# High products first where a stage starts beside the split of its activations

## The reference

```python
def first_block(x, ...):
    for l in range(DEPTH):                                  # DEPTH = 2
        n = rmsnorm(h, attn_norm[l])
        proj = n @ w_in[l]                                  # u, v_sgu, q, k, v_att
        y_sgu = sgu_mixer(gelu(u), gelu(v_sgu), ...)
        y_att = diff_attention(q, k, v_att, ...)
        h = h + concatenate([y_sgu, y_att]) @ w_out[l]
        h = h + conv_ffn(rmsnorm(h, ffn_norm[l]), w_up[l], conv_w[l], conv_b[l], w_down[l])
    return rmsnorm(h, final_norm)

def second_block(x, c, ...):
    h = modulate(rms_norm(x, pre_norm_mix), sh1, sc1)
    y = hybrid_mixer(h, w_in, ..., w_out)                   # concatenate([rnn, att]) @ w_out
    x = x + (1.0 + g1) * rms_norm(y, post_norm_mix)
    h = modulate(rms_norm(x, pre_norm_mlp), sh2, sc2)
    y = square(relu(h @ w_ff1)) @ w_ff2
    return x + (1.0 + g2) * rms_norm(y, post_norm_mlp)
```

## Time and profile before

| what | value |
|---|---|
| median of 3 runs | 1791.74 us |
| lowest and highest | 1791.13, 1794.27 us |
| the profiled execution's own time | 1788.96 us |
| its span, first to last instruction | 1787.2 us |
| TensorE busy | 1754.7 us, 98% of the span |
| weight loads (beside the matmuls) | 1432.7 us, 80% |
| VectorE, ScalarE, GpSimd busy | 63%, 44%, 58% |
| granted TensorE clock | 0.999 |

### The profile page before, as it was taken

The page is one execution under the profiler, slowest core; times in us unless marked ns, Lnnn a source line. Parts: engine busy times, 40 slices in busy tenths (PEclk is TensorE's granted clock), DMA queues, the critical chain, the costliest instruction groups (busy, mean ns, idle before and its releaser), DMA issues. The chain is left out here.

```text
span 1787.2 us, 26072 instructions
## 1 busy us (share of the span) xinstructions
PE 1754.7 (98%) x8977; PEld 1432.7 (80%) x8977; DVE 1123.3 (63%) x1827; ACT 779.9 (44%) x1271; POOL 1033.4 (58%) x1264
## 2 busy tenths in 40 slices
PE   8999999999999999999999999999999999999998
PEld 6876888888888887788888888877666788998886
DVE  4787666666656337766666665654586566666665
ACT  5445443333334335453333333456576654333332
POOL 6584555565465558265455564447411568888885
PEclk9999999999999999999999999999999999999999
DMA  7221223443423221133343332412301112233221
GB/s 256 95 104 51 98 88 132 153 162 109 152 94 118 95 98 57 48 107 118 141 164 137 131 119 94 142 50 96 117 1 49 48 53 90 99 115 116 97 95 47
DMA packets 103206, 184.70 MB, mean 103 GB/s; under 512 B 7322, under 2 KB 67404, under 8 KB 101068
## 3 DMA queue, kind: packets, MB, share of 16 engines
q1 hardware_dynamic: 102940, 183.44, 29.2%
q10 hardware_dynamic: 176, 0.07, 0.0%
HBM read 180.35 MB, written 2.10 MB: 102 GB/s over the span
## 5 line engine op out<-in xcount | busy, mean ns | idle before, releaser
L1003 POOL TENSOR_TENSOR w_lo<-raw,w_hi 128x256 fp32r<-128x256 f32 (+1 forms) x1124 | 908.1, 844 | 729.5 <-ACT w_hi L1087 723.3
L2513 PE MATMUL ps<-n_hi,w_hi 128*128 128x512 f32 (+1 forms) x1320 | 504.6, 382 | 2.0 <-issue 1.6
L2515 PE MATMUL ps<-n_hi,w_lo 128*128 128x512 f32 (+1 forms) x1320 | 499.0, 378 | 0.0
L2514 PE MATMUL ps<-n_lo,w_hi 128*128 128x512 f32 (+1 forms) x1320 | 498.7, 378 | 0.0
L1087 ACT ACTIVATE w_hi<-raw 128x1024 fp32r<-128x1024 f32 (+2 forms) x331 | 307.8, 938 | 356.0 <-PE ps L2515 237.9
L2513 PEld LDWEIGHTS ps<-n_hi,w_hi 128*128 128x128 f32 x1320 | 247.7, 188 | 51.1 <-issue 5.9
L2515 PEld LDWEIGHTS ps<-n_hi,w_lo 128*128 128x128 f32 x1320 | 247.6, 188 | 47.3
L2514 PEld LDWEIGHTS ps<-n_lo,w_hi 128*128 128x128 f32 x1320 | 247.9, 188 | 44.9 <-issue 0.2
L2050 DVE TENSOR_TENSOR ps<-ps,sq 128x512 f32<-128x512 f32 x88 | 61.3, 699 | 178.2 <-PE ps L2515 175.8
L2513 PE MATMUL ps<-x_hi,w_hi 128*128 128x512 f32 x416 | 166.9, 401 | 0.1
L2514 PE MATMUL ps<-x_lo,w_hi 128*128 128x512 f32 x416 | 162.2, 390 | 0.0
(11 more groups left out here) (362 smaller groups left out, 2662.7 us busy)
## 6 DMA issues: line engine op xcount, KB each, us to landing
raw<-in_w_up SPq DMA_DIRECT2D x44, 1024.0 KB, 7.0
raw<-in_w_ff SPq DMA_DIRECT2D x32, 1024.0 KB, 6.6
raw<-in_w_in SPq DMA_DIRECT2D x26, 1024.0 KB, 6.1
zb<-in_ada_w SPq DMA_DIRECT2D x16, 1536.0 KB, 8.5
raw<-in_w_down SPq DMA_DIRECT2D x44, 512.0 KB, 4.0
raw<-in_w_out SPq DMA_DIRECT2D x12, 1024.0 KB, 5.9
raw<-in_w_in SPq DMA_DIRECT2D x4, 512.0 KB, 8.3
za<-in_x SPq DMA_DIRECT2D x4, 512.0 KB, 6.2
```

The lines of the kernel that those rows point to most:

```text
L1003: last = pool.tensor_tensor(part[0], part[1], part[2], ALU.subtract)
L2513: pe.matmul(out, l_hi, r_hi, start=start, stop=False)
L2514: pe.matmul(out, l_hi, r_lo, start=False, stop=False)
L2515: return pe.matmul(out, l_lo, r_hi, start=False, stop=stop)
```

## The change

In the seven starts, a step that was "wait for the low half, then three matmuls for each open output" becomes "wait for the high half; for each open output the two matmuls with the high half; wait for the low half; for each open output the one matmul with the low half". The products and their number are the same, their order within a step is not. In `up` the new helper `pair` does this for two outputs, in `out2` the loop is written out, and the four banks of the first step are waited for together.

```diff
@@ features, for k in range(DT)
-                        pe.wait_ge(lo_ready, split + k + 1)
+                        c = slice(k * P, (k + 1) * P)
+                        pe.wait_ge(hi_ready, split + k + 1)
+                        for t in range(2):
+                            wh, wl = parts[t]
+                            pe.matmul(outs[t][:, :], wh[:, c], n_hi[:, k, :], start=k == 0, stop=False)
+                            pe.matmul(outs[t][:, :], wl[:, c], n_hi[:, k, :], start=False, stop=False)
+                        pe.wait_ge(lo_ready, split + k + 1)
                         for t in range(2):
-                            wh, wl = parts[t]
-                            last = product(outs[t][:, :], ...)
+                            last = pe.matmul(outs[t][:, :], parts[t][0][:, c], n_lo[:, k, :], start=False, stop=k == DT - 1)
                             if k == DT - 1:
                                 last.then_inc(quarter_done, 1)
@@ outa, for k in range(HT)
-                    pe.wait_ge(lo_ready, SPL["sub", l] + k + 1)
+                    pe.wait_ge(hi_ready, SPL["sub", l] + k + 1)
                     for m in range(4):
                         wh, wl = parts[m // 2]
                         c = k * 256 + m % 2 * P
-                        last = product(outs[m][:, :], ...)
+                        pe.matmul(outs[m][:, :], wh[:, c:c + P], n_hi[:, HT + k, :], start=k == 0, stop=False)
+                        pe.matmul(outs[m][:, :], wl[:, c:c + P], n_hi[:, HT + k, :], start=False, stop=False)
+                    pe.wait_ge(lo_ready, SPL["sub", l] + k + 1)
+                    for m in range(4):
+                        c = k * 256 + m % 2 * P
+                        last = pe.matmul(outs[m][:, :], parts[m // 2][0][:, c:c + P], n_lo[:, HT + k, :], start=False,
+                                         stop=k == HT - 1)
                         if k == HT - 1:
                             last.then_inc(quarter_done if m % 2 else full[BK["outa", l, m][0]], 1)
@@ up
+                    def pair(k, hi_made, lo_made):
+                        c = slice(k * P, (k + 1) * P)
+                        wh, wl = [[w_[:, (g + t) % 4, c] for t in range(2)] for w_ in (w_hi, w_lo)]
+                        pe.wait_ge(*hi_made)
+                        for t in range(2):
+                            pe.matmul(ps[t][:, :], wh[t], n_hi[:, k, :], start=k == 0, stop=False)
+                            pe.matmul(ps[t][:, :], wl[t], n_hi[:, k, :], start=False, stop=False)
+                        pe.wait_ge(*lo_made)
+                        for t in range(2):
+                            last = pe.matmul(ps[t][:, :], wh[t], n_lo[:, k, :], start=False, stop=k == DT - 1)
+                            if k == DT - 1:
+                                last.then_inc(quarter_done, 1)
...
-                            pe.wait_ge(lo_ready, split + k + 1)
-                            one(0, k)
-                            one(1, k)
+                            pair(k, (hi_ready, split + k + 1), (lo_ready, split + k + 1))
...
-                            pe.wait_ge(rawlo_ready, RAW[raw] + k + 1)
-                            one(0, k)
-                            one(1, k)
+                            pair(k, (rawhi_ready, RAW[raw] + k + 1), (rawlo_ready, RAW[raw] + k + 1))
@@ out2, for k in range(HT)
+                wh, wl = quarter(STR["out2",].g0 + k // 2)
+                outs = [bank(("out2", 0, t)) if k == 0 else ps[BK["out2", 0, t][0]] for t in range(NT)]
+                c = slice(k % 2 * S, k % 2 * S + S)
+                pe.wait_ge(hi_ready, SPL["att",] + k + 1)
+                for t in range(NT):
+                    pe.matmul(outs[t][:, :], n_hi[:, k, t * P:(t + 1) * P], wh[:, c], start=k == 0, stop=False)
+                    pe.matmul(outs[t][:, :], n_hi[:, k, t * P:(t + 1) * P], wl[:, c], start=False, stop=False)
                 pe.wait_ge(lo_ready, SPL["att",] + k + 1)
                 for t in range(NT):
-                    row_products("out2", ("out2", 0, t), 0, t, k, 1)
+                    last = pe.matmul(outs[t][:, :], n_lo[:, k, t * P:(t + 1) * P], wh[:, c], start=False, stop=k == HT - 1)
...
```

More of the change, by code:

```diff
@@ L2575, in features @@
                     for k in range(DT):
+                        c = slice(k * P, (k + 1) * P)
[4 more added lines that the diff above has]
+                            pe.matmul(outs[t][:, :], wl[:, c], n_hi[:, k, :], start=False, stop=False)
                         pe.wait_ge(lo_ready, split + k + 1)
                         for t in range(2):
-                            wh, wl = parts[t]
-                            last = product(outs[t][:, :], wh[:, k * P:(k + 1) * P], wl[:, k * P:(k + 1) * P],
-                                           n_hi[:, k, :], n_lo[:, k, :], k == 0, k == DT - 1)
+                            last = pe.matmul(outs[t][:, :], parts[t][0][:, c], n_lo[:, k, :], start=False, stop=k == DT - 1)
                             if k == DT - 1:
@@ L2814, in _ @@
                         c = k * 256 + m % 2 * P
-                        last = product(outs[m][:, :], wh[:, c:c + P], wl[:, c:c + P], n_hi[:, HT + k, :],
-                                       n_lo[:, HT + k, :], k == 0, k == HT - 1)
+                        pe.matmul(outs[m][:, :], wh[:, c:c + P], n_hi[:, HT + k, :], start=k == 0, stop=False)
[5 more added lines that the diff above has]
+                                         stop=k == HT - 1)
                         if k == HT - 1:
@@ L3145, in _ @@
             for k in range(HT):
+                wh, wl = quarter(STR["out2",].g0 + k // 2)
[5 more added lines that the diff above has]
+                    pe.matmul(outs[t][:, :], n_hi[:, k, t * P:(t + 1) * P], wl[:, c], start=False, stop=False)
                 pe.wait_ge(lo_ready, SPL["att",] + k + 1)
                 for t in range(NT):
-                    row_products("out2", ("out2", 0, t), 0, t, k, 1)
+                    last = pe.matmul(outs[t][:, :], n_lo[:, k, t * P:(t + 1) * P], wh[:, c], start=False, stop=k == HT - 1)
+                    if k == HT - 1:
+                        if t == NT - 1:
+                            last.then_inc(quarter_done, 2)
+                        else:
+                            last.then_inc(full[BK["out2", 0, t][0]], 1)
                 for f in ((0, 1), (2,), (3, 4), (5, 6))[k]:
```

## The result

| | kernel before | changed kernel |
|---|---|---|
| median, 22 runs each | 1791.07 us | 1793.89 us |
| lowest and highest | 1787.93, 1794.27 | 1791.41, 1798.60 |
| ratio of the medians, 95% interval | | 1.0017 (1.0011 to 1.0023) |
| profiled execution: span | 1787.2 us | 1794.7 us |
| profiled execution: granted TensorE clock | 0.999 | 0.997 |

The change costs 2.8 us, 0.17%; the forecast was 2.6 us, 0.14%, and 1794.3 us (on a median of three runs, which here, over 22, is 0.7 lower). But the two profiled executions lie 7.5 us apart, far more than the medians. So a part of what their traces show is not the change, and most of the experiments are about that part.

A forecast was written before the change was run, and what follows sets the result against it. TensorE, busy 98% of the span, was taken as the bound. Terms -0.51 - 0.27 + 2.72 + 0.65 = +2.59 us gave 1794.3 us on the median, 0.14% slower; range 1790.9 to 1796.4.

The forecast's parts named there:

- out-projection: `outa`, both layers: last step's first tile ends 1.36 us later, passing through a tight chain to `up`; +2.72 us.
- out2: Last step's first tile ends later; row gains shift and the last meets VectorE's second row update; +0.65 us (0 to 0.98).
- x_rnn: Start of `x_rnn`: first product no longer waits for the low half; gain 0.27 us.
- ff1: Start of ff1: first product no longer waits for the low half n_lo; gain 0.51 us.
- up: Start of `up`, both layers: released by GpSimd's w_lo, not the low halves, so gain nothing.
- waits in mid-step: The added wait in the middle of every changed step, already met, keeps the product pace; priced at nothing.
- stall of tile 4: Out-projection: tile 4 waits for tile 0's bank, 0.3 to 0.45 us, lying under the 1.36 us shift.
- the lock: At out2: VectorE and GpSimd lock each other out for a whole instruction; 0.9 us instead of 0.65.
- gains only: Rival: ScalarE or GpSimd catch up with the 1.36 us, leaving -0.78, 1791.0 us; chance 0.15.
- broken stream: Rival: mid-step waits make TensorE restart, 0.09 us in each of 44 steps, 4.0 us on top, 1798.3 us; chance 0.07.
- nothing that matters: Rival: low half almost never late and the tiles' shift absorbed, row updates included; 1791.7 us, chance 0.10.

The follow-up runs named there:

- e6: Kernel before plus a VectorE wait in the seven-products loop and repeated small matmuls before ff1, with the change in `outa` alone; 1791.86 us, ratio 1.0000.
- e7: Kernel before plus a VectorE wait in the seven-products loop and repeated small matmuls before ff1, with the change in out2 alone; 1790.29 us, ratio 0.9990.
- e11: Changed kernel with last steps of outa and out2 tile by tile, plus VectorE's loop wait, without repeated matmuls; 1788.54 us, 0.9977 of kernel before.
- e12: Changed kernel with last steps of outa and out2 tile by tile, VectorE's loop wait and repeated matmuls; 1787.32 us, 0.9964 of kernel before.
- e8: Same kernel as e12, run in an earlier group on the same chip; 1788.30 us, 0.9980 of kernel before.
- e3: Changed kernel plus a wait: VectorE's seventh-quarter low half follows GpSimd's sixth-quarter pieces in the seven-products loop; 1792.61 us, 0.9997 of kernel before.
- e2: Kernel before plus a wait: VectorE's seventh-quarter low half follows GpSimd's sixth-quarter pieces in the seven-products loop; 1789.64 us, ratio 0.9985.
- e1: Kernel before, unchanged, run again; 1792.73 us, ratio 0.9999.
- e9: Same kernel as e2, run again in another group; 1788.86 us, 0.9977 of kernel before.

## Why the prediction was right

The kernel got slower by the amount forecast, and the largest term, the out-projection, came link by link as forecast. The out2 term came near by luck: its amount fits, its collision was another one. Trace sizes come from the shifts of TensorE's starts.

| term | predicted | in the traces | from |
|---|---|---|---|
| out-projection, two layers | +2.72 | +2.61 | 1.32 and 1.29; e6 +3.04 by medians |
| out2 | +0.65 (0 to 0.98) | +0.82 | 2.82 less 2.00 in the table of shifts; e7 +0.84 |
| x_rnn | -0.27 | -0.25 | changed kernel, e11, and -0.27 in e12 |
| ff1 | -0.51 | -0.64 | e11 and e12 |
| up | 0 | 0 | |
| waits in mid-step | 0 | 0 | the pace kept within the changed stages; e8, e12 |
| sum | +2.59 | +2.54 (without falls of the clock) | medians +2.82, and +2.97 (2.3 to 3.6) without the stops |

*Out-projection:* every link moved by 1.3 to 1.4 as said. The stall of tile 4 (0.42) came, and lay under the rest as said. It is why the gap before `up` is 1.41 and not 1.8 to 2.0; the prediction gave about 1.5 for this case.

*out2:* the prediction let the second update of the pair run into the last gain, at 1.39 - 0.74 = 0.65. That did not happen: the update at 1428.31 took 0.74. The amount, 0.82, came from another collision, so that it lies in the range and near the 0.9 of the lock is luck. The last gains, 0.83 later where I had said 1.0, held up the small ss of 1425.52, a row that I had not read; the earlier trace rows leave it out. It passed on 0.62, and the first update, not the second, took 0.20 more. The Trainium skill, page "SBUF — State Buffer", section on who interferes with whom, has the loser of the shared port blocked for the whole instruction. The trace agrees here: ss takes 0.83 more, and ends 0.1 behind the first of the two gains (1425.31 and half of 2.54), as it did before.

*ff1:* I took the last small matmul to hold the array for 0.11 us. In e11 ff1's first product starts 0.03 behind it (1435.67, 1435.70), which makes 0.59, and 0.05 more come within the first steps; so it is near the 0.62 that I had given for a matmul that holds it for nothing.

*What I did not see* are two things that make single executions differ. My range held only because they strike both kernels. The gain at ff1 was swallowed in the profiled execution: from the second diagonal's transposes it is 8.12 us to ff1 in the changed kernel and 6.08 in e11, so the low clock took 2.04. I had read the 2.1 us wait for ss as a place where work is late, and not as a place where the clock may fall. And I set out from one profiled execution of 1788.96 us, 2.8 below the median of the runs shown, without asking what was different in it: it had one stop out of six, and three more would be 2.4 us. Whether the change makes the clock fall more often is open and could be part of what the medians have over the sum: a mean clock of 0.997 or less stood in 17 of the changed kernel's 22 executions, and in 42 of the 91 of the kernel before that ran beside the experiments; e3 has 7 of 11 and e2 5 of 11.

*Rivals:* gains only falls with e6, broken stream with e8 and e12 (it would have made them up to 4.0 us slower than their bases), nothing that matters with e3 against e2.

## What to carry to other kernels

Regrouping products over several open outputs moves the end of the first output: before the last step of such a group ask who waits for it, and keep that step tile by tile. A difference between two profiles is first to be split by stages, and a stage that differs far from the change is to be looked for in a second profile of the unchanged kernel. Where two engines share a port and one of them feeds the engine that bounds the kernel, a wait that orders them can be worth more than the change under study; here it cost nothing that the trace shows and brought 3.1 us.

## What the runs showed of the hardware

- VectorE's tensor_tensor with two operands in SBUF (1.23 us alone) and GpSimd's piece (about 0.7) never ran together. Which of them went first differed between rounds in which both stood in the same place to some hundredths of a microsecond: VectorE in one round of six in before's profile, in five of the changed kernel's, in six of e1's. The Trainium skill, page "SBUF — State Buffer", section on who interferes with whom, says that the one that issues first gets the port. By the listed starts VectorE issued 0.05 to 0.08 us before GpSimd's fourth piece in all these rounds, and GpSimd still went first in six of the eighteen. GpSimd's third piece ran on for 0.11 to 0.14 us behind VectorE's start, so both were waiting when it ended. In this situation the listed order does not decide, and the measurement stands.
- TensorE's clock fell to half behind a wait of 2.1 to 2.3 us with some small matmuls around it in four of seven profiles without the fillers (e2, e3, e9 and the changed kernel; not before, e1 and e11), and in none of seven with them. Behind the same waits it stayed up in e11 and fell in e9, so it is a chance. The price was 1.1 to 2.0 us in three of them and 0.04 in e3, by where it fell. The executions without a profile agree: a mean clock of 0.997 or less stood in 28 of the 54 of e1, e2, e3, e9 and e11, and in 1 of the 72 with the fillers. (Each profile also shows the half clock in its last 1.2 to 4.5 us, which lowers every mean a little.)
- It also fell at x_rnn in two of the fourteen profiles (e3 and e8), in e8 behind 9.00 us in which TensorE was busy for 8.92, and cost 1.4 to 1.5 us there; what brings it about was not tested.
